# Decay scale of the recurrence: from short operations on DVE between weight halves to a chain on GpSimd between its loads and its copies

## The chip, the core and the metric

The kernel runs on one core of a Trainium2 chip. The metric is the device time of one execution in microseconds, as the median of a few runs. The engines are TensorE (PE), VectorE (DVE), ScalarE (ACT), GpSimd (POOL) and SyncE (SP), which here only issues DMAs. Each engine runs its own instructions in order, and they meet only through semaphores: an instruction adds to one when it is done (`then_inc`), another waits for a value (`wait_ge`).

## What is computed

Two model blocks run one behind the other on 256 tokens of width 1024: a gated linear recurrence with an attention layer of a sliding window, then two feed-forward parts around two kinds of attention. Everything this text speaks of lies at the start, in the recurrence:

```python
u = rmsnorm(x, norm_g) @ w_in                       # x: 256 x 1024, w_in: 1024 x 3072
xb, gate = u[..., :1536], u[..., 1536:]
xb = causal_depthwise_conv(xb, conv_w, conv_b)      # 4 taps
r = sigmoid(blockwise(xb, wr) + br)                 # 16 blocks of 96 x 96
i = sigmoid(blockwise(xb, wi) + bi)
log_a = -8.0 * r * softplus(-lam)                   # lam: 1536 numbers
a = exp(log_a)
b = sqrt(-expm1(2.0 * log_a)) * (i * xb)
hs = scan(a, b);  y = hs * silu(gate);  x = x + y @ w_out
```

The decay scale is the factor `-8 * softplus(-lam) / 2`, one number for each of the 1536 channels, so 12 for each of the 128 partitions. The kernel works it out once, as `softplus(-lam) = max(-lam, 0) + log(1 + e)` with `e = exp(-|lam|)`, and the logarithm as a series in `z = e / (2 + e)`.

## The kernel before

The time goes into matmuls with weights of 32 bits. Each weight half (128 partitions x 1024 columns, 512 KB) is loaded by SP's queue into `stage`. ACT copies it in rounded form to `w_hi` (function `hi`), and DVE subtracts, `w_lo = stage - w_hi` (function `lo`, L1729). PE multiplies each product in three passes: `w_hi` by the high part of the activations, `w_hi` by their low part, `w_lo` by the high part (L595). Halves are numbered through the whole program; four of them have room in the ring `w_hi`/`w_lo`. `ring_free` says that PE is done with a half, `hi_done` that ACT's part is there, `w_done` that DVE's is.

The recurrence layer runs so. PE makes `xb` in six chunks of two 128-channel tiles (chunk `c`, two halves each). ACT moves the result out of PSUM with the first tap, DVE adds the other three taps (L1942, six instructions of about 0.4 us for a chunk), ACT writes the high part (`xb_hi`), DVE the low part (`xb_lo`, L1734). The 96-wide blocks of the gate weights don't fit 128-wide tiles. So they come in four groups of three tiles (`gates(g)` on PE): for each group two halves of 768 columns, which hold the gate weights. The halves of groups 0 and 1 are in `gate_st`, those of groups 2 and 3 in `arena`. Part of the input channels has to be brought to other partitions: that is POOL's function `stack(g)`, eight copies (L487) that wait one for another (semaphore `stack_done`) and, at their start, for `xbl` (DVE's low parts). PE's `gates(g)` first does 18 matmuls that need no stacked channels, then waits for `stack_done >= 8 * (g + 1)` and does 12 more (L825 and L827). Only behind these come the matmuls of the next chunk.

POOL's program around the change is: clear the gate buffers, issue the DMAs of the gate weights of groups 0 and 1 (L495, L503), then the first part of those of groups 2 and 3 (L495), `stack(0)`, `stack(1)`, the rest of the DMAs for groups 2 and 3 (L503) and 14 small DMAs, `stack(2)`, a square of the decay (L525), `stack(3)`.

DVE's program is a loop over halves, `for n in range(half_of(C_G + 2))`, written out by hand. In turn `n` it does `xb_lo` where a chunk ended one turn before, the taps where a chunk ends (`n` = 1, 3, 5, 7, 11, 15), `lo(n + 4)`, and then some of the decay scale's operations: `lam_ratio` in turns 3 to 5, `lam_series` in turns 6 to 10. There are 15 of them on DVE, all 128x12, and each waits for the one before (`lam_step`). ACT delivers `e` (semaphore `lam_e`) in its turn 2, and needs the finished factor (`lam_ready`) in its turn 12.

Of the kernel before, what the change touches and what calls it, by code (L numbers as in the profile page):

```python
# [11 lines left out]
ALU = mybir.AluOpType  # L12
# [9 lines left out]
LT = LRU // P  # L22
# [3 lines left out]
LRU_C = 8.0  # L26
# [49 lines left out]
CONV_W, CONV_B, BR, BI, LAM = 0, 48, 60, 72, 84  # L76
# [102 lines left out]
def build(nc, I, out):  # L179
    ctx = ExitStack()  # L180
    with ctx:
        def sb(name, shape, dt=F32):
            return ctx.enter_context(nc.sbuf_tensor(name, shape, dt))

        def sem(name):
            return ctx.enter_context(nc.semaphore(name))
# [14 lines left out]
        par_a = sb("par_a", [P, ROWS_A])  # L201
# [12 lines left out]
        lam = sb("lam", [P, 8, LT])  # L214
# [29 lines left out]
        def stacked(g, m):  # L244
# [16 lines left out]
        std_ready, rstd_ready, rb_ready, rb_sb = sem("std_ready"), sem("rstd_ready"), sem("rb_ready"), sem("rb_sb")  # L261
        xn_ready, xh_ready, xl_ready = sem("xn_ready"), sem("xh_ready"), sem("xl_ready")
        xh_second = sem("xh_second")
        par_t, par_ready, lam_e, lam_step, lam_ready = (
            sem(n) for n in ("par_t", "par_ready", "lam_e", "lam_step", "lam_ready"))
        conv_b, conv_s, conv_x, xbh, xbl = sem("conv_b"), sem("conv_s"), sem("conv_x"), sem("xbh"), sem("xbl")
        ri_sig = sem("ri_sig")
        lru_a, lru_t, lru_aa, lru_m, lru_s, lru_bx, lru_b, lru_h, lru_silu = (
# [204 lines left out]
        def _(pool):  # L473
# [7 lines left out]
            def stack(g):  # L481

                pool.wait_ge(xbl, (3 * g + 2) // 2 + 1)
                for i, (m, p, n, part, k, at) in enumerate(STACK):
                    if g or i:
                        pool.wait_ge(stack_done, len(STACK) * g + i)
                    pool.tensor_copy(stacked(g, m)[p:p + n, :], acts[at:at + n, 8 + 3 * g + k, part, :].bitcast(F32))\  # L487
                        .then_inc(stack_done, 1)

            for pair, place in enumerate((gate_st, gate_hi)):  # L490
                pool.wait_ge(set_done, 4 + pair)
                for w, name in enumerate(("a_gate_r_w", "a_gate_i_w")):
                    blocks = I[name][0].rearrange("(g b) i j -> b i g j", b=4)
                    for b, r, n, p, c in GATE_PIECES:
                        pool.dma_start(place[p:p + n, :, w, c:c + LB], blocks[b, r:r + n, 2 * pair:2 * pair + 2, :])\  # L495
                            .then_inc(gate_in[pair], 16)
                if pair == 1:
                    stack(0)
                    stack(1)
                for w, name in enumerate(("a_gate_r_w", "a_gate_i_w")):  # L500
                    blocks = I[name][0].rearrange("(g b) i j -> b i g j", b=4)
                    for b, r, n, p, c, j0, jn in GATE_AGAIN:
                        pool.dma_start(place[p:p + n, :, w, c:c + jn],  # L503
                                       blocks[b, r:r + n, 2 * pair:2 * pair + 2, j0:j0 + jn]).then_inc(gate_in[pair], 16)
# [1216 lines left out]
        def _(dve):  # L1721
# [149 lines left out]
                dve.wait_ge(xbh, c + 1)  # L1871
                low(8 + 2 * c, tiles(XB + 2 * c, 2), 2).then_inc(xbl, 1)

            e, den, z, z2, ser, big = (lam[:, j, :] for j in range(1, 7))

            def lam_after(step):

                dve.wait_ge(lam_step, step)

            def lam_ratio(n):  # L1880
                if n == 9:
                    dve.wait_ge(lam_e, 2)
                    dve.tensor_scalar(den, e, 2.0, 1.0, ALU.add, ALU.mult).then_inc(lam_step, 1)
                    dve.tensor_scalar(big, par_a[:, LAM:LAM + LT], -1.0, 0.0, ALU.mult, ALU.max).then_inc(lam_step, 1)
                if n == 10:
                    lam_after(2)
                    dve.reciprocal(z, den).then_inc(lam_step, 1)
                    lam_after(3)
                    dve.tensor_tensor(z, z, e, ALU.mult).then_inc(lam_step, 1)
                if n == 11:  # L1890
                    lam_after(4)
                    dve.tensor_tensor(z2, z, z, ALU.mult).then_inc(lam_step, 1)
                    lam_after(5)
                    dve.tensor_scalar(ser, z2, 1.0 / 15.0, 1.0, ALU.mult, ALU.mult).then_inc(lam_step, 1)

            def lam_series(n):
                if 12 <= n < 18:
                    lam_after(n - 6)
                    dve.scalar_tensor_tensor(ser, ser, 1.0 / (37 - 2 * n), z2, ALU.add, ALU.mult).then_inc(lam_step, 1)
                if n == 18:  # L1900
                    lam_after(12)
                    dve.scalar_tensor_tensor(ser, ser, 1.0, z, ALU.add, ALU.mult).then_inc(lam_step, 1)
                    lam_after(13)
                    dve.scalar_tensor_tensor(ser, ser, 2.0, big, ALU.mult, ALU.add).then_inc(lam_step, 1)
                if n == 19:
                    lam_after(14)
                    dve.tensor_scalar(lam[:, 7, :], ser, -LRU_C / 2, 1.0, ALU.mult, ALU.mult).then_inc(lam_ready, 1)

            x_end = {half_of(c) + 1: c for c in range(6)}
            def lru_gated(g):  # L1910

# [15 lines left out]
            for n in range(half_of(C_G + 2)):  # L1927
                if n - 1 in x_end:
                    xb_lo(x_end[n - 1])
                if n in (half_of(C_G) + 2, half_of(C_G + 1) + 2):  # L1930
                    gate_out((n - half_of(C_G)) // 4)
                if n in x_end:
                    c = x_end[n]
                    dve.wait_ge(conv_b, 2 * c + 2)
                    for tap in range(1, CONV):
                        for m in range(2):
                            t = 2 * c + m
                            x = tiles(XB + t)
                            if tap >= 2:
                                dve.wait_ge(conv_s, 4 * c + 2 * (tap - 2) + m + 1)  # L1940
                            w = CONV_W + (CONV - 1 - tap) * LT + t
                            dve.scalar_tensor_tensor(x[:, tap:T], bank[4 + c % 2][:, m * T:(m + 1) * T - tap],  # L1942
                                                     par_a[:, w:w + 1], x[:, tap:T], ALU.mult, ALU.add)\
                                .then_inc(conv_x if tap == CONV - 1 else conv_s, 1)
                    if c == 0:
                        lo(4)
                if n:
                    lo(n + 4)
                lam_ratio(n + 6)
                if n in (6, 7, 8):  # L1950
                    lam_series(2 * n)
                    lam_series(2 * n + 1)
                if n in (9, 10):
                    lam_series(n + 9)
                if n in (14, 16):
                    lru_gated(n // 2 - 7)
                if n in (18, 20):
                    lru_square(n // 2 - 9)
                if n == 20:
                    lru_gated(2)  # L1960
                if n == 23:
                    lru_square(2)
# [401 lines left out]
            for r in range(NH + 5):  # L2364
# [9 lines left out]
                if r < NH:  # L2374
                    n = r
# [13 lines left out]
                if 2 <= r < NH + 2:  # L2389
                    n = r - 2  # L2390
# [117 lines left out]
```

## Time and profile before

| | |
|---|---|
| median of 3 runs | 786.79 us (786.68 to 787.05) |
| the profiled execution's own time | 786.78 us |
| span of its trace | 784.9 us |
| PE busy | 776.7 us, 99% of the span |
| DVE busy | 585.6 us, 75% |
| ACT busy | 488.0 us, 62% |
| POOL busy | 106.9 us, 14%, nearly all of it in the first 200 us |

The time of an execution is 1.9 us longer than the span of its trace; what lies around the span is not in the trace. A group's or an instruction's row begins with its start and its duration. PE's instructions overlap: a matmul of 256 columns has a duration of 0.28 us in the records, but the next one starts 0.12 us behind it. So the busy share says little of PE, and short stops are read from the starts. Every stretch of this trace has the granted clock 1.00.

### The profile page before, as it was taken

The numbers are of one execution on the slowest core, as the hardware profiler recorded it, in microseconds if no ns is written. First come the engines' busy times: TensorE is split into PE (matmuls) and PEld (weight loads), VectorE is DVE, ScalarE is ACT, GpSimd is POOL, SyncE is SP. The second block draws the span as 40 slices with busy tenths as digits, with TensorE's granted clock in tenths as the row PEclk, the third lists the DMA queues.
The fourth block names the chain that finished last, engine by engine and source line by source line (L and its number), as shares of the span: only waits on it lengthen the run. The fifth ranks groups of instructions, "written<-read, shape, count | busy, mean of one in ns | idle before, by whom it ended". The sixth has DMA issues, their size and how long they took to land.

```text
span 784.9 us, 14573 instructions
## 1 busy us (share of the span) xinstructions
PE 776.7 (99%) x5321; PEld 711.4 (91%) x5321; DVE 585.6 (75%) x892; ACT 488.0 (62%) x761; POOL 106.9 (14%) x195
## 2 busy tenths in 40 slices
PE   9999999999999999999999999999999999999997
PEld 8999999998998888888888899999999888888885
DVE  5989997978868887776459664796588887787443
ACT  7799946788675655554346565764756665555334
POOL 9697100157100000000000031000000000000000
PEclk9999999999999999999999999999999999999999
DMA  8663565633646766666665544445555676665651
GB/s 264 188 181 118 171 212 161 211 112 110 188 126 181 226 191 187 187 195 202 190 189 163 185 147 151 127 144 161 182 165 157 195 213 189 195 184 184 195 178 54
DMA packets 101557, 136.57 MB, mean 174 GB/s; under 512 B 5320, under 2 KB 86912, under 8 KB 101504
## 3 DMA queue, kind: packets, MB, share of 16 engines
q1 hardware_dynamic: 99232, 133.23, 55.4%
q0 software_dynamic: 2112, 2.54, 1.3%
q8 instruction: 35, 0.57, 0.3%
q14 instruction: 18, 0.15, 0.1%
q10 hardware_dynamic: 160, 0.07, 0.1%
HBM read 134.78 MB, written 1.05 MB: 173 GB/s over the span
## 4 chain that ended last, share of the span: by engine, by line
PE 91%; DVE 4%; ACT 3%; issue 1%; DMA 0%; ACTq 0%
PE bank L595 30%; PE bank L658 20%; PE bank L660 11%; PE bank L603 8%; PE bank L704 8%; PE bank L751 5%; PE bank L752 3%; DVE w_lo L1729 2%; DVE arena L1942 1%; PE bank L945 1%; PE bank L927 1%; ACT arena L1216 1%; PE bank L952 1%; ACT w_hi L1216 1%; ACT acts L1216 1%
## 5 line engine op out<-in xcount | busy, mean ns | idle before, releaser
L1729 DVE TENSOR_TENSOR w_lo<-stage,w_hi 128x1024 fp32r<-128x1024 f32 x249 | 305.3, 1231 | 124.5 <-ACT w_hi L1216 123.9
L1216 ACT ACTIVATE w_hi<-stage 128x1024 fp32r<-128x1024 f32 (+1 forms) x251 | 262.5, 1052 | 117.5 <-PE bank L595 41.7
L595 PE MATMUL bank<-acts,w_hi 128*128 128x256 f32 x1520 | 277.6, 285 | 0.9 <-DVE w_lo L1729 0.4
L658 PE MATMUL bank<-acts,w_hi 128*128 128x512 f32 x704 | 244.8, 392 | 0.0
L595 PEld LDWEIGHTS bank<-acts,w_hi 128*128 128x128 f32 x1520 | 236.5, 192 | 3.6 <-issue 1.7
L595 PE MATMUL bank<-acts,w_lo 128*128 128x256 f32 x760 | 214.9, 283 | 0.0
L660 PE MATMUL bank<-acts,w_lo 128*128 128x256 f32 x704 | 197.2, 280 | 0.0
L658 PEld LDWEIGHTS bank<-acts,w_hi 128*128 128x128 f32 x704 | 131.7, 187 | 29.2
L595 PEld LDWEIGHTS bank<-acts,w_lo 128*128 128x128 f32 x760 | 145.6, 192 | 0.0
L660 PEld LDWEIGHTS bank<-acts,w_lo 128*128 128x128 f32 x704 | 133.1, 189 | 0.0
L1216 ACT ACTIVATE arena<-bank 128x512 f32<-128x512 f32 (+1 forms) x79 | 43.6, 561 | 63.6 <-PE bank L660 45.9
L603 PE MATMUL bank<-w_hi,acts 128*128 128x256 f32 (+1 forms) x320 | 71.8, 319 | 0.4 <-DVE w_lo L1729 0.4
L555 POOL TENSOR_SCALAR arena<-arena,rden 128x128 f32<-128x128 f32 (+1 forms) x44 | 23.5, 547 | 283.7 <-DVE rden L2106 283.1
L751 PE MATMUL bank<-acts,w_hi 128*128 (+1 forms) x176 | 61.1, 391 | 0.0
L1216 ACT ACTIVATE acts<-arena 128x512 fp32r<-128x512 f32 (+3 forms) x41 | 26.4, 644 | 53.2 <-DVE arena L2260 32.9
L1216 ACT ACTIVATE arena<-arena 128x512 f32<-128x512 f32 (+3 forms) x64 | 38.4, 605 | 29.7 <-DVE arena L2236 14.5
L603 PEld LDWEIGHTS bank<-w_hi,acts 128*128 128x128 f32 x320 | 52.2, 191 | 4.6 <-DVE w_lo L1729 0.8
L704 PE MATMUL bank<-w_hi,acts 128*128 128x512 f32 x176 | 54.4, 390 | 0.0
L603 PE MATMUL bank<-w_lo,acts 128*128 128x256 f32 (+1 forms) x160 | 50.4, 315 | 0.0
L752 PE MATMUL bank<-acts,w_lo 128*128 (+1 forms) x176 | 49.3, 280 | 0.0
L2228 DVE TENSOR_TENSOR arena<-arena,bank 128x512 f32<-128x512 f32 x44 | 30.2, 685 | 22.2 <-ACT arena L1216 22.2
L751 PEld LDWEIGHTS bank<-acts,w_hi 128*128 128x128 f32 x176 | 32.9, 187 | 7.2
(221 smaller groups left out, 810.2 us busy)
## 6 DMA issues: line engine op xcount, KB each, us to landing
stage<-ffn_w_gate SPq DMA_DIRECT2D x44, 512.0 KB, 4.2
stage<-ffn_w_up SPq DMA_DIRECT2D x44, 512.0 KB, 4.4
stage<-ffn_w_down SPq DMA_DIRECT2D x44, 512.0 KB, 3.8
stage<-w_in SPq DMA_DIRECT2D x40, 512.0 KB, 3.6
stage<-a_w_in SPq DMA_DIRECT2D x24, 512.0 KB, 4.6
stage<-b_w_in SPq DMA_DIRECT2D x16, 512.0 KB, 3.7
stage<-a_w_out SPq DMA_DIRECT2D x12, 512.0 KB, 3.7
stage<-b_w_out SPq DMA_DIRECT2D x8, 512.0 KB, 3.5
```

The source lines that it names most:

```text
L555: pool.tensor_scalar(s, s, rden[:, 2 * n + q:2 * n + q + 1], 1.0, ALU.mult, ALU.mult).then_inc(p_norm, 1)
L595: mm = pe.matmul(dst, w[:, slot, c:c + P], a[:, k, :] if isinstance(k, int) else a[:, bass.ds(k, 1), :], start=start and n == 0, stop=stop ...
L603: mm = pe.matmul(dst, a[:, k, tb * P:(tb + 1) * P], w[:, slot, c:c + n], start=start and i == 0, stop=stop and i == 2, skip_group_check=True)
L658: pe.matmul(two[p][:, m, :], w_hi[:, half % RING, c:c + P], wide(acts[:, k, :, :]), start=k == 0, stop=False, skip_group_check=True)
L660: mm = pe.matmul(two[p][:, m, 0:T], w_lo[:, half % RING, c:c + P], a_hi[:, k, :], start=False, stop=k == KD - 1, skip_group_check=True)
L704: mm = pe.matmul(token_bank(tb, h)[:, :], a[:, k, t], w[:, slot, c], start=False, stop=w is w_hi and a is a_hi, skip_group_check=True)
L751: pe.matmul(b[:, :], w_hi[:, half % RING, w], both, start=start, stop=False, skip_group_check=True)
L752: return pe.matmul(b[:, 0:T], w_lo[:, half % RING, w], high, start=False, stop=stop, skip_group_check=True)
L927: mm = pe.matmul(bank[score_bank(n + i)][:, c:c + w], q[r, t * T + c:t * T + c + P], k[r, 0:keys], start=True, stop=True)
L1216: return nc.scalar.activation(out_, in_, func, **kw)
L1729: dve.tensor_tensor(w_lo[:, n % RING, 0:w], src, w_hi[:, n % RING, 0:w].bitcast(F32), ALU.subtract)\
L2228: dve.tensor_tensor(y, y, two[ffn_two(n, j, u)][:, :, 0:T], ALU.add).then_inc(ff_add, 1)
```

## The change

The 15 operations on DVE go away except the reciprocal. That one stands in turn 5 now, behind `lo(9)`, and waits for POOL (`lam_den`). All the others are done by POOL in the new function `decay_scale()`, which is called once, between the DMAs of `pair == 1` and `stack(0)`. The steps are written with two-operand and one-operand instructions in place of the fused ones, so there are more of them: two before the reciprocal, 17 behind it. Each waits for its predecessor, by `pool.wait_ge(lam_step, ...)`.

```diff
@@ POOL @@
+            def decay_scale():
+                steps = [0]
+                def step(op):
+                    steps[0] += 1
+                    op.then_inc(lam_step, 1)
+                    pool.wait_ge(lam_step, steps[0])
+                e, den, z, z2, ser, big = (lam[:, j, :] for j in range(1, 7))
+                pool.wait_ge(lam_e, 2)
+                pool.tensor_scalar(den, e, 2.0, 1.0, ALU.add, ALU.mult).then_inc(lam_den, 1)
+                step(pool.tensor_scalar(big, par_a[:, LAM:LAM + LT], LRU_C / 2, 0.0, ALU.mult, ALU.min))
+                pool.wait_ge(lam_inv, 1)
+                step(pool.tensor_tensor(z, z, e, ALU.mult))
+                step(pool.tensor_tensor(z2, z, z, ALU.mult))
+                step(pool.tensor_scalar(ser, z2, 1.0 / 15.0, 1.0 / 13.0, ALU.mult, ALU.add))
+                for n in (11, 9, 7, 5, 3):
+                    step(pool.tensor_tensor(ser, ser, z2, ALU.mult))
+                    step(pool.tensor_scalar(ser, ser, 1.0 / n, 1.0, ALU.add, ALU.mult))
+                step(pool.tensor_tensor(ser, ser, z2, ALU.mult))
+                step(pool.tensor_scalar(ser, ser, 1.0, -LRU_C, ALU.add, ALU.mult))
+                step(pool.tensor_tensor(ser, ser, z, ALU.mult))
+                pool.tensor_tensor(lam[:, 7, :], ser, big, ALU.add).then_inc(lam_ready, 1)
...
                 if pair == 1:
+                    decay_scale()
                     stack(0)
                     stack(1)
@@ DVE, loop over n @@
                 if n:
                     lo(n + 4)
-                lam_ratio(n + 6)
-                if n in (6, 7, 8):
-                    lam_series(2 * n)
-                    lam_series(2 * n + 1)
-                if n in (9, 10):
-                    lam_series(n + 9)
+                if n == 5:
+                    dve.wait_ge(lam_den, 1)
+                    dve.reciprocal(lam[:, 3, :], lam[:, 2, :]).then_inc(lam_inv, 1)
```

POOL's program, from its last DMA of the gate weights to `stack(0)` and the start of `stack(1)` (`lam` is the small tile of the decay scale, `acts` the activations that PE reads). Before:

```order
L495 DMA arena<-a_gate_i_w 96x2x96
L487 CAST acts<-acts 32x256 [waits xbl]
L487 CAST acts<-acts 32x256 [waits stack_done] x3
L487 CAST acts<-acts 64x256 [waits stack_done] x4
L487 CAST acts<-acts 32x256 [waits stack_done,xbl]
```

And now (from the first of these rows to the fifth step; behind them the same pair of operations comes four times more, then the last four steps, and then `stack(0)` as before):

```order
L520 DMA arena<-a_gate_i_w 96x2x96
L501 ISA
L501 TENSOR_SCALAR lam<-lam 128x12 [waits lam_e]
L502 TENSOR_SCALAR lam<-par_a 128x12
L504 TENSOR_TENSOR lam<-lam 128x12 [waits lam_inv,lam_step]
L505 TENSOR_TENSOR lam<-lam 128x12 [waits lam_step]
L506 TENSOR_SCALAR lam<-lam 128x12 [waits lam_step]
L508 TENSOR_TENSOR lam<-lam 128x12 [waits lam_step]
L509 TENSOR_SCALAR lam<-lam 128x12 [waits lam_step]
```

`stack(0)` stood directly behind the DMAs; now 19 operations on `lam` stand ahead of it, and the third of them waits for DVE's reciprocal.

DVE's program, turns 4 to 6 of its loop (`gate_st` rows are `lo(8)` and `lo(9)`). Before:

```order
L1734 TENSOR_TENSOR acts<-arena,acts 128x2x256 [waits xbh]
L1729 TENSOR_TENSOR w_lo<-gate_st,w_hi 128x768 [waits hi_done]
L1887 RECIPROCAL lam<-lam 128x12 [waits lam_step]
L1889 TENSOR_TENSOR lam<-lam 128x12 [waits lam_step]
L1942 SCALAR_TENSOR_TENSOR arena<-bank,par_a,arena 128x255 [waits conv_b]
L1942 SCALAR_TENSOR_TENSOR arena<-bank,par_a,arena 128x255
L1942 SCALAR_TENSOR_TENSOR arena<-bank,par_a,arena 128x254 [waits conv_s] x2
L1942 SCALAR_TENSOR_TENSOR arena<-bank,par_a,arena 128x253 [waits conv_s] x2
L1729 TENSOR_TENSOR w_lo<-gate_st,w_hi 128x768 [waits hi_done]
L1892 TENSOR_TENSOR lam<-lam 128x12 [waits lam_step]
L1894 TENSOR_SCALAR lam<-lam 128x12 [waits lam_step]
L1734 TENSOR_TENSOR acts<-arena,acts 128x2x256 [waits xbh]
```

And now:

```order
L1760 TENSOR_TENSOR acts<-arena,acts 128x2x256 [waits xbh]
L1755 TENSOR_TENSOR w_lo<-gate_st,w_hi 128x768 [waits hi_done]
L1933 SCALAR_TENSOR_TENSOR arena<-bank,par_a,arena 128x255 [waits conv_b]
L1933 SCALAR_TENSOR_TENSOR arena<-bank,par_a,arena 128x255
L1933 SCALAR_TENSOR_TENSOR arena<-bank,par_a,arena 128x254 [waits conv_s] x2
L1933 SCALAR_TENSOR_TENSOR arena<-bank,par_a,arena 128x253 [waits conv_s] x2
L1755 TENSOR_TENSOR w_lo<-gate_st,w_hi 128x768 [waits hi_done]
L1942 RECIPROCAL lam<-lam 128x12 [waits lam_den]
L1760 TENSOR_TENSOR acts<-arena,acts 128x2x256 [waits xbh]
```

The reciprocal moved behind a chunk's six taps and the second gate half: from in front of the first L1942 here to the place where L1892 stood. PE's and ACT's programs have the same instructions in the same order as before.

## Rows read from the trace of the kernel before

**Rows 1.** The page's first part: busy time, share of the span, instructions.
```profile
PE 776.7 (99%) x5321; PEld 711.4 (91%) x5321; DVE 585.6 (75%) x892; ACT 488.0 (62%) x761; POOL 106.9 (14%) x195
```

**Rows 2.** Waits of the weight loads, 16 to 130 us: total, times, longest.
```profile
PEld bank L595 <- DVE w_lo L1729: 0.8, 2, 0.6
```

**Rows 3.** PE in order of time, around its two stops.
```profile
41.61 0.28 PE L595 MATMUL bank<-acts,w_lo 128*128 128x256 f32 x1
41.95 0.50 PE L595 MATMUL bank<-acts,w_hi 128*128 128x256 f32 x2
...
60.99 0.28 PE L595 MATMUL bank<-acts,w_lo 128*128 128x256 f32 x1
61.65 0.50 PE L595 MATMUL bank<-acts,w_hi 128*128 128x256 f32 x2 [0.38 <-DVE w_lo L1729]
```

**Rows 4.** PE where `gates(0)` begins its last 12 matmuls.
```profile
37.41 0.28 PE L825 MATMUL bank<-acts,w_hi 128*128 128x256 f32 x1
```

**Rows 5.** POOL in order of time; idle time in brackets.
```profile
30.95 5.13 POOL L487 CAST acts<-acts 32x256 fp32r<-32x256 f32 x8 [5.94 <-DVE acts L1734]
36.69 5.46 POOL L487 CAST acts<-acts 32x256 fp32r<-32x256 f32 x8 [0.61 <-DVE acts L1734]
```

**Rows 6.** DVE in order of time, turns 3 to 6.
```profile
30.05 0.17 DVE L1883 TENSOR_SCALAR lam<-lam 128x12 f32<-128x12 f32 x1
30.20 0.69 DVE L1734 TENSOR_TENSOR acts<-arena,acts 128x512 fp32r<-128x512 f32 x1
...
31.67 0.22 DVE L1887 RECIPROCAL lam<-lam 128x12 f32<-128x12 f32 x1
32.01 2.42 DVE L1942 SCALAR_TENSOR_TENSOR arena<-bank,par_a,arena 128x255 f32<-128x255 f32 x6
...
35.22 0.40 DVE L1892 TENSOR_TENSOR lam<-lam 128x12 f32<-128x12 f32 x1
35.73 0.90 DVE L1734 TENSOR_TENSOR acts<-arena,acts 128x512 fp32r<-128x512 f32 x1
36.55 1.21 DVE L1729 TENSOR_TENSOR w_lo<-stage,w_hi 128x1024 fp32r<-128x1024 f32 x1
```

**Rows 7.** POOL, other stretches: short operations, and copies behind one another.
```profile
155.46 0.18 POOL L561 COPY arena<-sink 128x1 f32<-128x1 f32 x1
155.72 0.41 POOL L574 TENSOR_SCALAR arena<-con 128x256 f32<-128x256 f32 x1
71.09 1.47 POOL L525 TENSOR_TENSOR arena<-arena 128x768 f32<-128x768 f32 x1
30.95 2.43 POOL L487 CAST acts<-acts 32x256 fp32r<-32x256 f32 x4 [5.94 <-DVE acts L1734]
30.95 1.05 POOL L487 CAST acts<-acts 32x256 fp32r<-32x256 f32 x1 [5.94 <-DVE acts L1734]
36.69 1.33 POOL L487 CAST acts<-acts 32x256 fp32r<-32x256 f32 x1 [0.61 <-DVE acts L1734]
```

**Rows 8.** ACT in order of time.
```profile
24.24 0.21 ACT L1216 ACTIVATE lam<-lam 128x12 f32<-128x12 f32 x1
35.95 1.01 ACT L1216 ACTIVATE arena<-bank,par_a 128x256 f32<-128x256 f32 x2
40.63 0.63 ACT L1216 ACTIVATE acts<-arena 128x512 fp32r<-128x512 f32 x1 [2.72 <-DVE arena L1942]
```

**Rows 9.** PE's first matmuls, in order of time.
```profile
3.08 1.06 PE L783 MATMUL bank<-ones 128*128 128x128 f32 x4
5.93 0.87 PE L794 MATMUL bank<-con,arena 128*128 128x128 f32 x5
6.42 0.82 PE L794 MATMUL bank<-con,arena 128*128 128x128 f32 x6
```

**Rows 10.** All instructions of these lines: duration in ns, least/median/most.
```profile
L783 PE MATMUL bank<-ones x22: 275/421/581, 1.0 to 8.1; 128*128 128x128 f32 x22
L794 PE MATMUL bank<-con,arena x16: 272/273/474, 5.2 to 7.4; 128*128 128x128 f32 x16
```

More of the change, by code:

```diff
@@ L263, in build @@
         xh_second = sem("xh_second")
-        par_t, par_ready, lam_e, lam_step, lam_ready = (
-            sem(n) for n in ("par_t", "par_ready", "lam_e", "lam_step", "lam_ready"))
+        par_t, par_ready, lam_e, lam_den, lam_inv, lam_step, lam_ready = (
+            sem(n) for n in ("par_t", "par_ready", "lam_e", "lam_den", "lam_inv", "lam_step", "lam_ready"))
         conv_b, conv_s, conv_x, xbh, xbl = sem("conv_b"), sem("conv_s"), sem("conv_x"), sem("xbh"), sem("xbl")
@@ L1872, in xb_lo @@
                 low(8 + 2 * c, tiles(XB + 2 * c, 2), 2).then_inc(xbl, 1)
[L1874 to L1907, printed above, removed]
             x_end = {half_of(c) + 1: c for c in range(6)}
```

## The prediction

> **What bounds the kernel now.** I read the busy shares first: PE is at work for 776.7 us of the span and DVE for 585.6 [rows 1], so time is lost or won only where PE starts late. The waits of PE's weight loads come next. Between 16 and 130 us, the stretch of the changed code, PE stopped twice for `w_lo`, 0.8 us together [rows 2]. In PE's order of time the size of both is seen by the starts, which are 0.12 us apart for each matmul when nothing is late: from 41.61 the next would start at 41.73 and starts at 41.95, 0.22 us late; from 60.99 it would be 61.11 and is 61.65, 0.54 us late [rows 3]. So 0.76 us is all that lighter work on DVE can give back here, however much it is lighter.
>
> The opposite question is what can make PE late. POOL's order of time shows it: `stack(0)` starts at 30.95, when DVE's low parts are there, and takes 5.13 us, to 36.08 [rows 5]. PE reaches the matmuls that wait for it at 37.41 [rows 4]. That is a margin of 1.3 us, on an engine that looks idle at 14% busy. The gap of 5.94 us before `stack(0)` [rows 5] ends where `stack(0)` begins, so what is put there must be done by about 31, or by 32.3 with the margin.
>
> **The change part by part.** *When the chain on POOL can go on.* Two of its operations need only ACT's `e`, which is there at 24.45 [rows 8], and fall into the gap, at no cost. The third waits for DVE's reciprocal, and DVE has this now in turn 5, where L1892 stood: 35.22 in this trace [rows 6]. DVE gets there earlier by what is taken out before: two operations of `lam`, from 30.05 to 30.20, 0.15 us, and the reciprocal with the product, from 31.67 to 32.01, 0.34 us [rows 6]. So the reciprocal starts at 34.73 and is done, at 0.22 us [rows 6], at 34.95. By then the time at which `stack(0)` used to be three quarters done has passed, and 17 steps follow.
>
> *What a step costs.* POOL has no 128x12 operation in the trace. The lower bound is a copy of one column, 0.18 us. The upper one is a dependent copy of 256 columns in `stack(0)`: four took 2.43 and the first of them 1.05, so 0.46 us each [rows 7]. A 256-column operation lasts 0.41 [rows 7], so the wait between two steps is 0.05. The number of columns matters little at 12: (0.41 - 0.18) x 12/255 is 0.01 for one operand, (1.47 - 0.18) x 12/767 is 0.02 for two [rows 7]. I take 0.18 + 0.05 + 0.02 = 0.25 us, near the lower bound, since 12 columns are nearer to one than to 256. Alone, 17 steps would take 4.3 us.
>
> *What stands in their way.* The first copy of `stack(1)`, 0.41 us of work, took 1.33 us from 36.69 [rows 7], while DVE was in L1729 from 36.55 for 1.21 us, and the first copy of `stack(0)` took 1.05. The reverse is seen at 35.22 and 35.73, where DVE's 0.17 us operation took 0.40 and L1734 0.90 instead of 0.69 [rows 6] beside POOL's last copies. So POOL and DVE's instructions with two inputs in SBUF exclude one another, and POOL gets about one operation in at each boundary. The Trainium skill, GPSIMD Engine Reference, section "Key points", says that GpSimd shares its SBUF interfaces with VectorE and contends with instructions that have two SBUF inputs. By that rule the steps stop under L1734 and L1729, and the trace agrees with the 1.33 us; without it the chain would end 3 us sooner (a rival below).
>
> DVE after the reciprocal: `xb_lo(2)` 34.95 to 35.6, `lo(10)` to 36.75, six taps to 39.1 (2.4 us, input in PSUM, not in the way; ACT's first tap at 35.95 [rows 8] would be half a microsecond sooner), `lo(11)` to 40.3, `xb_lo(3)` to 40.95. POOL's steps: one at 35.6, nine in the 2.35 us of taps, one at 40.3, the last six behind 40.95, 1.5 us: the chain ends at 42.45. DVE is idle by then, since `lo(12)` needs a slot of the ring that PE holds. So `stack(0)` runs unhindered, 8 x 0.46 = 3.7 us, to 46.2.
>
> *PE's stop.* PE gets to L825 at 37.41 as before and stands until 46.2: 8.8 us. Behind the waiting matmul everything of PE is queued, and ACT and DVE wait for the ring in turn. Nothing of it comes back later, since PE is busy to the end. The two stops of before go away, 0.76 us: DVE is done with `lo(11)` long before, and the second one came from ACT, which waited 2.72 us for DVE's taps before 40.63 [rows 8] and now has time to spare. `stack(1)` follows `stack(0)` in about 5.4 us [rows 5], to 51.6, and `gates(1)` needs it some 9.4 us behind `gates(0)`, since PE's order between the two is unchanged. `lam_ready` comes at 42.45, while ACT needs it only behind work that waits for PE; it costs nothing.
>
> *PE after the stop.* No stretch of this trace shows a granted clock under 1.00. But PE's own rows show two paces. In its first microseconds, coming from idle, four records of 128 columns took 1.06 us, so (1.06 - 0.42)/3 = 0.21 us apart; from 6.42 on six took 0.82, (0.82 - 0.27)/5 = 0.11 apart [rows 9, 10]. That is the ratio of the two levels, 1.2 and 2.4 GHz. PE had worked since 1.00, and the five records from 5.93, at 0.15 apart [rows 9], straddle the change. So a slow stretch of about 5.2 us, which costs half of itself, 2.6 us. An 8.8 us stop is longer than any that this trace has behind the start; that the clock falls in it is an estimate from the start alone. Bounds: nothing, and 2.6 plus the same spread again if the rise comes late, 3.5 us. I take 2.6. The Trainium skill, "TensorE: Matmul & The Clock Gate", section "What's actually happening", says the array is at half its clock by default and that activity releases it; by that rule the price is paid after this stop too, and the start of this trace agrees.
>
> *Sum.* The profiled execution took 786.78 us, 0.01 from the median of 786.79. 786.8 + 8.8 - 0.8 + 2.6 = 797.4 us.
>
> **Rivals.**
> - *POOL and DVE don't hinder each other here.* The steps run from 35.0 to 39.3, `stack(0)` takes 3.7 to 5.13, the stop ends between 43.0 and 44.4, so it is 5.6 to 7.0 us long. Time: 786.8 + 6.3 - 0.8 + 2.6 = 794.9. Against it: the 1.33 and 0.40 us rows.
> - *A step costs as much as a copy of `stack`, 0.46 us.* One at 35.6, five in the taps, one at 40.3, ten behind 40.95: 45.55, and 49.3 with `stack(0)`, a stop of 11.9. Time 800.5. For it: each step is a round trip through a semaphore, which I priced from one pair of rows.
> - *The clock stays up.* The same stop without 2.6: 794.8.
> - *The other side, faster.* If `stack(0)` were done by 37.41, only the 0.76 us would count and the time would be 786.0. With 3.7 us for the copies the chain must end by 33.7, and at 17 steps of 0.25 the reciprocal must be done by 29.4. In DVE's order it stands behind `lo(9)`, at 34.95. Even steps that cost nothing would put the end at 38.7, 1.3 us late. It needs an order other than the printed one.
> - *Code for the arithmetic has to be loaded on POOL.* The program has an instruction L501 ISA in front of the first step. The Trainium skill, GPSIMD Engine Reference, section "Instruction dispatch", has an instruction-memory load of about 6 us at the first call of a freshly loaded kernel. In the two operations before the reciprocal it would be hidden by the gap from 25 to 34.95; only paid at the first two-operand step would it count. Worked from rows, bounded by the gap before `stack(0)`, 5.94 us [rows 5], as a length that the present order can hide: 797.4 + 5.9 = 803.3.
>
> **How the numbers follow.** Forecast as worked out 0.60; POOL unhindered 0.13; dear steps 0.12; clock stays up 0.10; code load 0.02; faster 0.02; none of these 0.01. The single time is that of the forecast, 797.4. The range, 792.8 to 801.0, holds the forecast, nearly all of the first and third rivals, and dear steps; outside are the code load, a short stop joined with a high clock (786.8 + 5.6 - 0.8 = 791.6) and the faster side. A change within 0.2% (1.6 us) can't be told from none. Slower by more than that: 0.96. Within it: 0.02. Faster by more than that would need 1.6 us, where 0.76 can be had: 0.02 for what I have overlooked.
>
> **What would show it.** PE's starts jump once, at L825 in `gates(0)`, from about 37.4 to about 46, released by POOL's `stack(0)`. POOL's `lam` operations: two near 25, then nothing until about 35, then 17 with holes under DVE's L1755 and L1760. PE's granted clock is under 1.00 in the microseconds behind the stop and the starts are 0.21 apart there. The stops of before at 41.95 and 61.65 have no counterpart. From there to the end each row stands later by the same amount. It would be wrong if `stack(0)` still ended before 37.41, if the steps ran evenly through L1755, if a second stop came at `gates(1)`, `gates(2)` or `gates(3)`, or if later stretches gave the time back.

## The result and the profile after

| | before | after |
|---|---|---|
| median | 786.79 us (786.68 to 787.05) | 796.35 us (795.76 to 796.73) |
| profiled execution | 786.78 us, span 784.9 | 795.76 us, span 794.0 |

The changed kernel is slower: the ratio is 1.0121, 95% interval 1.0106 to 1.0136. Its page begins with these lines (busy time, share, instructions), which answer to [rows 1]:

```profile
PE 777.4 (98%) x5321; PEld 712.4 (90%) x5321; DVE 583.8 (74%) x878; ACT 488.3 (62%) x761; POOL 112.6 (14%) x214
```

PE does the same work, DVE 1.8 us less, POOL 5.7 more. Nothing of 9 us is to be seen there; it is in where PE stands still. First its waits over the whole execution (total, times, longest), which answer to [rows 2]:

```profile
PE bank L851 <- POOL acts L487: 8.4, 1, 8.4
```

Then its instructions in order of time, which answer to [rows 3, 4]. L851 is L825 of before, L621 is L595:

```profile
37.09 0.28 PE L621 MATMUL bank<-acts,w_lo 128*128 128x256 f32 x1
45.80 0.58 PE L851 MATMUL bank<-acts,w_hi 128*128 128x256 f32 x1 [8.43 <-POOL acts L487]
46.18 0.41 PE L853 MATMUL bank<-acts,w_lo 128*128 128x256 f32 x1
46.40 0.41 PE L851 MATMUL bank<-acts,w_hi 128*128 128x256 f32 x1
```

One stop, at the place where `gates(0)` waits for `stack(0)`: due at 37.21, begun at 45.80, 8.59 us late. The next matmul starts 0.38 us behind it, and from there on the starts are 0.21 us apart where they should be 0.12. The granted clock (the first number behind the engines' busy times) says why:

```profile
42.00:43.00 1.00, 0.00 (x0) 0.00 (x0) 0.00 (x0) 0.00 (x0) 0.93 (x3) 0.74 1.02 358
43.00:44.00 1.00, 0.00 (x0) 0.00 (x0) 0.00 (x0) 0.00 (x0) 0.81 (x4) 0.50 0.08 27
...
49.00:49.20 0.20, 0.20 (x3) 0.20 (x3) 0.20 (x1) 0.20 (x1) 0.20 (x1) 0.50 0.00 0
49.20:49.40 0.20, 0.20 (x3) 0.20 (x3) 0.18 (x1) 0.20 (x1) 0.20 (x1) 0.74 0.00 0
49.40:49.60 0.20, 0.20 (x4) 0.20 (x4) 0.00 (x0) 0.20 (x1) 0.20 (x1) 1.00 0.00 0
```

It fell to the half level, 1.2 GHz, in the middle of 42 to 43 us, while PE stood, and rose near 49.3. POOL's order of time shows what PE waited for; these answer to [rows 5, 7]:

```profile
26.57 0.27 POOL L502 TENSOR_SCALAR lam<-par_a 128x12 f32<-128x12 f32 x1
34.89 0.46 POOL L504 TENSOR_TENSOR lam<-lam 128x12 f32<-128x12 f32 x1 [8.05 <-DVE lam L1942]
35.43 1.24 POOL L505 TENSOR_TENSOR lam<-lam 128x12 f32<-128x12 f32 x1
36.76 0.20 POOL L506 TENSOR_SCALAR lam<-lam 128x12 f32<-128x12 f32 x1
37.04 0.22 POOL L508 TENSOR_TENSOR lam<-lam 128x12 f32<-128x12 f32 x1
...
39.10 1.05 POOL L509 TENSOR_SCALAR lam<-lam 128x12 f32<-128x12 f32 x1
40.23 0.53 POOL L508 TENSOR_TENSOR lam<-lam 128x12 f32<-128x12 f32 x1
...
42.01 0.21 POOL L513 TENSOR_TENSOR lam<-lam 128x12 f32<-128x12 f32 x1
42.16 7.95 POOL L487 CAST acts<-acts 32x256 fp32r<-32x256 f32 x16
```

POOL stood 8.05 us for the reciprocal, did its 17 steps from 34.89 to 42.2, and then began the copies that used to begin at 30.95. DVE's rows, which answer to [rows 6]:

```profile
34.52 0.22 DVE L1942 RECIPROCAL lam<-lam 128x12 f32<-128x12 f32 x1
34.66 0.63 DVE L1760 TENSOR_TENSOR acts<-arena,acts 128x512 fp32r<-128x512 f32 x1
35.38 1.23 DVE L1755 TENSOR_TENSOR w_lo<-stage,w_hi 128x1024 fp32r<-128x1024 f32 x1
```

**The account.** I take for each PE instruction between 17 and 150 us how much later it started than 0.12 us for each matmul behind the one before. In the kernel before the two stops come to 0.95 us (0.76 at the stops, 0.19 more at the instructions just behind them). In the one after they are gone, the new stop is 8.59 and the slow stretch 1.63. PE also reached this part 0.2 us earlier (17.70 in place of 17.90). -0.95 + 8.59 + 1.63 - 0.2 = 9.07 us; the spans differ by 9.1. So in the profiled execution nothing is left to explain, and nothing was given back later. The median is 0.6 us longer than this execution. The spans of the other three are 0.4 to 0.8 us longer, at mean granted clocks of 0.992 to 0.994 where this one has 0.995; they left no trace that would show where.

### The profile page after: what moved, and what is told of

Its sections match the earlier page's. It is cut to its first block, busy times and chain, and to the rows that moved or that the text cites. A ratio compares the mean times of both kernels' runs of the same rounds, so it can differ in the third digit from the quotient of the medians.

```text
span 794.0 us, 14579 instructions
## 1 busy us (share of the span) xinstructions
PE 777.4 (98%) x5321; PEld 712.4 (90%) x5321; DVE 583.8 (74%) x878; ACT 488.3 (62%) x761; POOL 112.6 (14%) x214
## 3 DMA queue, kind: packets, MB, share of 16 engines
HBM read 134.78 MB, written 1.05 MB: 171 GB/s over the span
## 4 chain that ended last, share of the span: by engine, by line
PE 93%; DVE 3%; ACT 1%; POOL 1%; DMA 1%; issue 1%; SPq 0%; ACTq 0%; POOLq 0%
PE bank L621 32%; PE bank L684 20%; PE bank L686 11%; PE bank L629 8%; PE bank L730 8%; PE bank L777 5%; PE bank L778 3%; PE bank L971 1%; PE bank L953 1%; DVE w_lo L1755 1%; PE bank L978 1%; ACT acts L1242 1%; DMA arena<-x 1%; DVE arena L1933 1%; PE bank L851 0%
## 5 line engine op out<-in xcount | busy, mean ns | idle before, releaser
L621 PE MATMUL bank<-acts,w_hi 128*128 128x256 f32 x1520 | 277.6, 285 | 0.4 <-DVE acts L1867 0.3
L621 PEld LDWEIGHTS bank<-acts,w_hi 128*128 128x128 f32 x1520 | 236.9, 192 | 2.7 <-issue 1.7
L621 PE MATMUL bank<-acts,w_lo 128*128 128x256 f32 x760 | 215.1, 283 | 0.0
L621 PEld LDWEIGHTS bank<-acts,w_lo 128*128 128x128 f32 x760 | 145.8, 192 | 0.0
L778 PE MATMUL bank<-acts,w_lo 128*128 (+1 forms) x176 | 49.3, 280 | 0.0
```

Of the source, the lines that this page charges most:

```text
L621: mm = pe.matmul(dst, w[:, slot, c:c + P], a[:, k, :] if isinstance(k, int) else a[:, bass.ds(k, 1), :], start=start and n == 0, stop=stop ...
L778: return pe.matmul(b[:, 0:T], w_lo[:, half % RING, w], high, start=False, stop=stop, skip_group_check=True)
```

## The experiments

**The reciprocal sooner, twice.** The first theory was that the loss is the lateness of `stack(0)` and nothing else. The edit in the changed kernel (the second one has `n == 2`):

```diff
-                if n == 5:
+                if n == 3:
                     dve.wait_ge(lam_den, 1)
                     dve.reciprocal(lam[:, 3, :], lam[:, 2, :]).then_inc(lam_inv, 1)
```

Turn 3:

> Edit: the changed kernel with DVE's reciprocal in turn 3 of its loop in place of turn 5 (about 29.8 in place of 34.5 us). Nothing else moves. Theory (PE waits for stack(0), which waits for the 17 steps): the steps start near 30.1, one gets in at each boundary of DVE's two-input instructions and eight in the taps, the chain ends near 37.9, stack(0) near 42.4, PE's stop at gates(0) is about 5.2 us in place of 8.6. Time 791.1 us if TensorE's clock stays up, 792.7 if it falls (in the changed kernel it fell 5.3 us into the stop, so this is at the edge). Rival (the loss comes from the POOL operations as such or from POOL hindering DVE, wherever they stand): time stays near 796.

Turn 2:

> Edit: the changed kernel with DVE's reciprocal in turn 2 of its loop (about 26.6 us, just after POOL's first operation). Theory: the chain starts near 26.9 and ends near 33.1, stack(0) near 37.6 to 38.2, PE's stop is 0.4 to 1.0 us, the clock stays up, and the two old stops are gone (0.95): time 786.2 to 787.5, most likely 786.7, so no difference from before. Rival (the steps cost by themselves): near 796. If the steps hinder DVE as well, its weight halves come late and stops appear at 41 or 61 us: 787.5 to 789.

Measured: 794.43 us for turn 3 (1.0095, interval 1.0078 to 1.0111), 791.51 for turn 2 (1.0061, 1.0044 to 1.0078). Each move forward made it faster with the same operations on the same engines, so the rival that these cost about 9 us wherever they stand falls. But both sizes were missed, the second by nearly 5 us. PE's stop was 6.21 us in the one and 4.27 in the other, against 5.2 and 0.4 to 1.0 expected. POOL's rows of turn 2 show the reason:

```profile
28.49 0.20 POOL L509 TENSOR_SCALAR lam<-lam 128x12 f32<-128x12 f32 x1
28.78 2.76 POOL L508 TENSOR_TENSOR lam<-lam 128x12 f32<-128x12 f32 x1
31.62 0.20 POOL L509 TENSOR_SCALAR lam<-lam 128x12 f32<-128x12 f32 x1
...
33.66 1.69 POOL L512 TENSOR_TENSOR lam<-lam 128x12 f32<-128x12 f32 x1
35.43 0.21 POOL L513 TENSOR_TENSOR lam<-lam 128x12 f32<-128x12 f32 x1
```

and DVE's rows beside them:

```profile
28.79 1.21 DVE L1755 TENSOR_TENSOR w_lo<-stage,w_hi 128x1024 fp32r<-128x1024 f32 x1
29.92 0.68 DVE L1760 TENSOR_TENSOR acts<-arena,acts 128x512 fp32r<-128x512 f32 x1
30.52 0.94 DVE L1755 TENSOR_TENSOR w_lo<-gate_st,w_hi 128x768 fp32r<-128x768 f32 x1
31.39 2.42 DVE L1933 SCALAR_TENSOR_TENSOR arena<-bank,par_a,arena 128x255 f32<-128x255 f32 x6
```

A step of 0.21 us took 2.76: it met three DVE instructions with two inputs in SBUF that stand back to back, and waited for all three, to 31.46. It did not get in at the boundary of two of them, as the prediction had supposed. The next hold, 1.69 us, is two such instructions long (33.73 to 35.27). In the taps L1933, which read PSUM, steps go by at 0.29 us each.

The clock was the other miss. It fell in both kernels, and in turn 3 the slow stretch cost 2.59 us, in turn 2 1.56. Account: -0.95 + 6.21 + 2.59 = 7.85 against spans 7.9 apart; -0.95 + 4.27 + 1.56 - 0.23 (an earlier start) = 4.65 against 4.7.

**Ten steps fewer.** In `decay_scale()`:

```diff
-                for n in (11, 9, 7, 5, 3):
+                for n in ():
```

> Leaves out the five pairs of operations of the series' loop (so the decay scale is another number); 7 steps behind the reciprocal in place of 17. Theory: ten steps of 0.29 us and the hole of about 1.2 us among them go, the chain ends near 38.2, stack(0), now hindered by DVE's two-input instructions at 38.9 to 40.7, near 43.4: stop 6.2 us, the clock falls late in it and costs about 1 us: 793.0 us. Rival (the round trip to DVE's reciprocal and the first load of the arithmetic cost most, the steps little): 795 to 796.

Measured: 794.06 us (1.0092, 1.0075 to 1.0109), stop 6.09, slow stretch 1.85, -0.95 + 6.09 + 1.85 = 6.99 against 7.0. The chain ended at 38.34 in place of 42.22, 3.9 us sooner, and the stop is 2.5 us shorter: `stack(0)` began under DVE's two-input instructions now and took 5.1 us, where it took 3.6 when DVE was idle. The time is 1.1 us over the one expected, of which the clock is 0.85 (1.85 and not 1). Ten of the 17 steps taken out gave back 2.3 of the 9.6 us. With seven left PE still stood for 6 us, because the chain still begins only at 35.1, behind the reciprocal; the move of the reciprocal to turn 2, with all 17 steps, gave back 4.8.

**PE kept at work in the stop.** Between PE's first matmuls of `gates(0)` and its wait, PE multiplies ones by ones (`warm(36)`; the trace shows each call as two records). The result is not used:

```diff
+                if g == 0:
+                    pe.wait_ge(conv_x, 6)
+                    warm(36)
                 pe.wait_ge(stack_done, len(STACK) * (g + 1))
```

> Edit: the changed kernel, with 36 matmuls of ones by ones (128 columns, their result unused, as at the program's start) on TensorE between the first 18 matmuls of gates(0) and its wait for stack(0). They take about 7.9 us of the 8.6 us stop. Theory (the stop costs 8.6 us and 1.6 us more because the clock falls in it): PE goes on at 45.8 as before, granted clock 1.00 throughout, time 796.35 - 1.6 = 794.7 us. Rival (the 1.6 us behind the stop are another start-up cost, or the clock is nothing to the time): 796.3. If stack(0) is what PE waits for, the time can't fall under 794.5.

Measured: 795.82 us (1.0113, 1.0096 to 1.013). The clock part of the theory is borne out: it is 1.00 in every stretch from 17 to 130 us, also behind the stop. The time is not: 795.82 where 794.7 was expected, since two other things happened. PE's rows:

```profile
37.40 8.20 PE L809 MATMUL bank<-ones 128*128 128x128 f32 x72
46.59 0.39 PE L854 MATMUL bank<-acts,w_hi 128*128 128x256 f32 x1 [0.99 <-POOL acts L487]
...
70.95 0.50 PE L621 MATMUL bank<-acts,w_hi 128*128 128x256 f32 x2 [0.72 <-DVE w_lo L1758]
```

One POOL step was held for 1.95 us instead of 1.05 and the useful matmuls were due at 37.40 and came at 46.59, 9.19 us late. And a stop of 0.98 us at `lo(19)` came back, at the place of the old one at 61.65. DVE needed 2.20 us for this half, where it took 0.94 in the changed kernel, next to a POOL operation that had begun 0.08 us sooner:

```profile
68.62 1.46 POOL L551 TENSOR_TENSOR arena<-arena 128x768 f32<-128x768 f32 x1
68.70 2.20 DVE L1758 TENSOR_TENSOR w_lo<-arena,w_hi 128x768 fp32r<-128x768 f32 x1
```

-0.95 + 9.19 + 0.1 + 0.98 = 9.3 us, as the spans are apart. So the slow stretch went away as the theory has it, and two holds between POOL and DVE, of 0.6 and 0.98 us, took its place. This run shows that the clock falls because PE stands, and it does not show by itself what the fall costs: that is read from the starts of the matmuls in the other traces.

**The steps behind the copies.** The first two operations stay in the gap, the other 17 go behind `stack(1)`. The function is split in two (`next(scale)` is the first two operations, `next(scale, None)` the 17 steps), and the steps wait for the last copy:

```diff
-                    decay_scale()
+                    scale = decay_scale()
+                    next(scale)
                     stack(0)
                     stack(1)
+                    next(scale, None)
```

> Edit: the changed kernel with the two first POOL operations in the gap as now, but the 17 steps behind stack(0) and stack(1), ahead of POOL's further DMAs. Theory (only the place of the steps costs): PE goes through gates(0) at 37.4 without a stop; the steps run from about 42 to 48 us, lam_ready is 1 to 2 us late for ACT, the gate weights' last DMAs land near 57 where ACT wants them at 55, and stack(2) ends near 65.5 where PE wants it at 62.7: one or more new stops near 61 to 66 us of 2 to 4 us together, 789 to 790.5 us. Rival (17 operations on POOL cost their time wherever they stand): 795 to 796.

Measured: 796.16 us (1.0124, 1.0108 to 1.0139), as slow as the changed kernel and 6 us over the theory. By the number alone the rival had won, and only the trace says otherwise: PE goes through `gates(0)` without a stop and has two others. Its waits:

```profile
PE bank L855 <- POOL acts L487: 3.3, 1, 3.3
PE bank L625 <- DVE w_lo L1759: 3.1, 1, 3.1
```

The second of these begins in ACT's program:

```profile
45.77 1.06 ACT L1246 ACTIVATE w_hi<-stage 128x1024 fp32r<-128x1024 f32 x1
51.33 3.07 ACT L1246 ACTIVATE arena<-arena,lam 128x256 f32<-128x256 f32 x6 [4.49 <-POOL lam L515]
```

ACT stood 4.49 us for the decay scale, which was ready at 51.3; I had put it at about 48. The copies are why. The steps could begin only at 44.47, since `stack(1)`, which ended at 42.15 in the kernel before, ended at 44.4 here. One of its copies, begun at 39.16, was held by four DVE instructions with two inputs in SBUF that follow one another at once:

```profile
39.16 3.84 POOL L487 CAST acts<-acts 64x256 fp32r<-64x256 f32 x1
```

```profile
39.20 1.21 DVE L1759 TENSOR_TENSOR w_lo<-stage,w_hi 128x1024 fp32r<-128x1024 f32 x1
40.33 0.68 DVE L1764 TENSOR_TENSOR acts<-arena,acts 128x512 fp32r<-128x512 f32 x1
40.93 1.81 DVE L1759 TENSOR_TENSOR w_lo<-gate_st,w_hi 128x768 fp32r<-128x768 f32 x2
```

In the kernel before, two short operations stand behind the first of these four (at 41.82) and two behind the third (at 43.77). With ACT stood the rounded weight halves behind it in ACT's queue, so PE stood 3.30 us at 57.26. The other is `stack(2)`, behind POOL's DMAs, 3.46 us at 70.21. Slow stretches of 1.54 and 1.49 us follow. -0.95 + 3.30 + 1.54 + 3.46 + 1.49 = 8.8 of 9.0.

**The gap used for DMAs.** As before, with POOL's eight DMAs of gate weights (4.5 us) moved from behind `stack(1)` to the gap ahead of `stack(0)`:

```diff
+                    next(scale)
                 for w, name in enumerate(("a_gate_r_w", "a_gate_i_w")):
...
+                if pair == 1:
+                    stack(0)
+                    stack(1)
+                    next(scale, None)
```

> Edit: as the one before, and in the gap before stack(0) POOL issues the eight DMAs of gate weights (4.5 us) that came behind stack(1). Theory: stack(0) starts near 31.3 in place of 30.95 and is inside its margin; the weights land early; the steps end near 48, the small DMAs and stack(2) come as early as before; ACT gets lam_ready up to 1.5 us late, which can leave one stop of 0 to 1 us near 61. Time 785.9 to 786.8, most likely 786.3, so the gain of at most 0.95 us at last, or no difference. Rival: 788 or more, if POOL's steps hinder DVE's weight halves behind 42 us.

Measured: 791.09 us (1.0056, 1.0042 to 1.007), over 4 us more than expected. The stop for `stack(2)` is gone, the one for ACT's `lam_ready` is the same 3.30 us (the copy of 3.84 us is here too, at 39.22), and one of 1.78 us appeared at 65.97, for `lo(19)`; -0.95 + 3.30 + 0.07 + 1.78 + 0.10 = 4.3, as the spans. So the 17 steps cost 4.3 us here and 9.6 in the changed kernel, by who waits behind them. No place I tried on POOL is free.

**How much DVE's relief is worth.** In the kernel before, DVE does one of its 15 operations:

```diff
-                lam_ratio(n + 6)
-                if n in (6, 7, 8):
-                    lam_series(2 * n)
-                    lam_series(2 * n + 1)
-                if n in (9, 10):
-                    lam_series(n + 9)
+                if n == 10:
+                    dve.wait_ge(lam_e, 2)
+                    dve.tensor_scalar(lam[:, 7, :], lam[:, 1, :], -LRU_C / 2, 1.0, ALU.mult, ALU.mult).then_inc(lam_ready, 1)
```

> Leaves out the decay scale's series: DVE does one operation in turn 10 in place of 15, so the factor is another number. Upper bound of what taking the work off DVE can give. Theory: the two stops go and nothing else changes, 785.8 us (0.95 less than before). Rival (DVE's 3 us of short operations are worth their time): 783.8.

Measured: 786.93 us (ratio 1.0003, 0.9994 to 1.0012). Neither theory holds. The two old stops are gone as I said, and three others have come, 0.28 at 37.59, 0.57 at 71.99 and 0.30 at 76.61, which with -0.95 make the 0.2 us by which the spans differ. Two of them are PE waiting for POOL's copies:

```profile
37.29 0.28 PE L595 MATMUL bank<-acts,w_lo 128*128 128x256 f32 x1
37.59 0.39 PE L825 MATMUL bank<-acts,w_hi 128*128 128x256 f32 x1
...
71.99 0.39 PE L825 MATMUL bank<-acts,w_hi 128*128 128x256 f32 x1 [0.31 <-POOL acts L487]
```

POOL's copies of `stack(0)` in this kernel, and DVE's rows beside them:

```profile
33.75 3.33 POOL L487 CAST acts<-acts 64x256 fp32r<-64x256 f32 x2
```

```profile
33.86 0.94 DVE L1729 TENSOR_TENSOR w_lo<-gate_st,w_hi 128x768 fp32r<-128x768 f32 x1
34.73 0.68 DVE L1734 TENSOR_TENSOR acts<-arena,acts 128x512 fp32r<-128x512 f32 x1
35.59 1.22 DVE L1729 TENSOR_TENSOR w_lo<-stage,w_hi 128x1024 fp32r<-128x1024 f32 x1 [0.18 <-ACT w_hi L1216]
```

Two copies of 0.41 us took 3.33. In the kernel before, the two at the same place (34.36) took 1.72, and there DVE had its short operations between L1729 and L1734 [rows 6]. From this comes a theory: the work taken off DVE was also what let POOL in.

**The same with turns 5 and 6 moved.** In the kernel before, nothing left out:

```diff
-                lam_ratio(n + 6)
+                lam_ratio({3: 9, 4: 10, 7: 11}.get(n, 0))
+                for k in {7: (12, 13), 8: (14, 15, 16), 9: (17, 18), 10: (19,)}.get(n, ()):
+                    lam_series(k)
```

> Edit: the kernel before, all of the decay scale on DVE, but the two operations of turn 5 and the two of turn 6 moved to turn 7 and behind (turn 7: four, turn 8: three, turn 9: three, turn 10: one), so that they follow lo(11) instead of preceding it. Theory (the two stops of the kernel before come from DVE's 1.5 us of short operations ahead of lo(11)): PE's stop at 41.95 goes away, ACT gets chunk 3 about 1 us sooner, the stop at 61.65 shrinks or goes: 785.8 to 786.2 us. Rival (the stops come from ACT or from POOL's use of the port): 786.8 as before.

Measured: 787.15 us, so slower, if by little (1.0011, 1.0002 to 1.002). The stop at 41.95 is gone, one of 0.30 at 37.60 is there, and the one of 61.65 is 0.97 in place of 0.64: its `lo(19)` took 2.21 us, begun at 59.71 next to POOL's L525, where it took 1.30 before. Two of the 11 executions took 789.06 and 789.34 us, at a granted clock of 0.999 and more; none of these has a trace, and the median does not hang on them.

From these two I formed the theory of openings, and two kernels test it. One leaves turns 3 to 5 as they were and moves only turn 6's pair:

```diff
-                if n in (6, 7, 8):
-                    lam_series(2 * n)
-                    lam_series(2 * n + 1)
-                if n in (9, 10):
-                    lam_series(n + 9)
+                for k in {7: (12, 13, 14), 8: (15, 16, 17), 9: (18,), 10: (19,)}.get(n, ()):
+                    lam_series(k)
```

> Edit: the kernel before, with only the two operations of turn 6 moved to turns 7 and 8 (turn 7: three, turn 8: three, turns 9 and 10: one each); turns 3 to 5 keep their six. New theory (POOL's copies get the port only where DVE's two-input instructions don't follow one another at once, and the short operations of turns 3 to 5 are such places): stack(0) ends near 36.1 again, there is no stop at 37.6, lo(11) is 0.5 us sooner, so the stop at 41.95 goes, and the stop near 61.7 is between 0.1 and 1.0 us: 786.2 to 787.0. Old theory (every short operation off DVE's path ahead of lo(11) gains): 786.0. Rival (stack(0) is late in the two kernels before by chance): 787.1 as dve_later.

The other leaves out the series (the same five lines go) and keeps `lam_ratio` in turns 3 to 5:

```diff
+                if n == 10:
+                    lam_after(6)
+                    dve.tensor_scalar(lam[:, 7, :], ser, -LRU_C / 2, 1.0, ALU.mult, ALU.mult).then_inc(lam_ready, 1)
```

> Leaves out the decay scale's series from turn 6 on, as dve_light (so the factor is another number), but keeps the six short operations of turns 3 to 5 where they stood. New theory: these six work as openings for POOL's copies, so stack(0) ends near 36.1 and PE's stop at 37.6 (0.28 us in dve_light) is gone although DVE has more to do; the stop at 41.95 is gone too: 786.2 to 786.7, less than dve_light's 786.93 by 0.3 us or so. Rival (more work on DVE can only cost): 786.9 to 787.3.

Measured: 786.37 us for the first (0.9995, 0.9986 to 1.0004), 786.69 for the second (1.0, 0.9991 to 1.0009). In both, `stack(0)` takes 5.13 and 5.14 us as before, and there is no stop at 37.6 and none at 41.95; left are 0.53 and 0.89 us near 61.3. `stack(0)` of the first kernel, to be held against [rows 5]:

```profile
30.98 5.13 POOL L487 CAST acts<-acts 32x256 fp32r<-32x256 f32 x8 [5.96 <-DVE acts L1734]
```

For the traces this bears the theory out: with six more operations on DVE, the second kernel has lost `dve_light`'s stop at `stack(0)`. The two that count are those of turn 5, between L1729 and L1734: `dve_later` keeps turns 3 and 4 and has the stop, these two kernels keep turn 5 as well and don't. As times, 786.69 against 786.93 is no more than a leaning, since the two intervals overlap. The first, `dve_mid`, is the best kernel of the study: its 11 runs lie between 786.30 and 786.64, the 21 of the kernel before between 786.46 and 786.95. The interval of the ratio still includes 1. In its trace -0.95 + 0.53 is the 0.4 us by which its span is shorter.

## Why the prediction was right

797.4 us were predicted and 796.35 measured, in the range of 792.8 to 801.0. By its steps:

1. *POOL reaches the chain's third operation only behind DVE's turn 5, at 34.95.* Measured: the reciprocal ended at 34.74, in a trace that runs 0.2 us earlier there. Right.
2. *A step costs 0.25 us.* Measured 0.20 to 0.22 as duration and 0.29 from start to start. Too cheap by 0.04, for 17 steps 0.7 us.
3. *DVE's two-input instructions hold the chain; it ends at 42.45.* It ended at 42.22. That it comes so near is luck, since two errors cancel: of 7.5 us in all I had 3.25 for holds, and the four long steps show 0.25 + 1.03 + 0.85 + 0.32 = 2.45 (over 0.21 each). The mechanism as I put it, one operation at each boundary, was wrong where several such instructions follow one another (2.76 us for one step with the reciprocal in turn 2). In the changed kernel it happened to matter little: eight of the 17 steps fell into the taps, and five came when DVE was done (from 40.85).
4. *`stack(0)` runs unhindered, 3.7 us.* Measured 3.6 (42.16 to 45.8), and DVE was idle from 40.7 to 48.4. Right.
5. *A stop of 8.8 us, one place.* 8.59 us, at L851. Right.
6. *A slow clock behind it, 2.6 us.* Right in kind, 1.0 us too dear in the profiled execution: 1.63. This is the term that was mis-sized. It was read from one slow stretch of 5.2 us at the start [rows 9, 10]. But the clock fell at 42.5, while PE still stood, and rose at 49.3, so only 3.5 us of PE's work, from 45.8, ran slow. Where PE worked longer before the rise, it cost more: 4.1 us for 1.85 in `short_series`, 5.7 us for 2.59 in `recip_turn3` (rises at 47.55 and 49.34). The other stops cost 1.56, 1.54 and 1.49, and in `dmas_in_gap` nothing.
7. *The old stops go, 0.76 us, and nothing comes back.* 0.95 with the instructions just behind them. That ACT and DVE were ahead of PE during the stop is seen in DVE's idle time of 7.73 us before 48.42. The later rows are all 9.1 us later.

The sum was 10.6 us over before; the profiled execution is 9.0 over and the median 9.6. Step 6 is 1.0 of the difference, steps 5 and 7 are 0.2 each, the earlier start of PE is 0.2.

The rivals: that POOL and DVE don't hinder one another is refuted by 1.24 and 1.05 us for single steps. Steps of 0.46 are refuted by 0.29. The clock did fall. There was no load of code in the chain: behind the wait, the first arithmetic with two operands took 0.46 us, and the operation at 25.11, the first on POOL, 1.39, both far below the 5.9 us of that rival, the latter inside the gap.

What the text took for granted and the runs don't bear out stands in its first part: that 0.76 us is what lighter work on DVE gives back. DVE's short operations were not only a cost ahead of `lo(11)`; between two long instructions they also let POOL through. Without them, in `dve_light`, 0.95 us of old stops turned into 1.15 us of new ones.

What stays open is when the clock falls. `behind_stacks` and `dmas_in_gap` have nearly the same stop, and only in one did it fall (below). The traces show that it differs, not why. Open is also why executions of one kernel differ, by 1 us in the changed kernel and by 2.4 us in `dve_later`.

## What to carry to other kernels

An idle stretch of a helper engine has a deadline, which is what stands behind it in that engine's queue. Before work is put in, look for the last input it waits for, not only for its length: here a gap of 5.9 us was there for a chain whose input came 4 us after its end. Here an engine at 14% had 1.3 us of margin for 17 steps and became the one that PE waited for, while PE's two waits for the one at 75% had come to 0.8 us in this part [rows 2].

When instructions of two engines exclude one another, short operations between long ones are openings for the other engine. Taking them out can move the wait to the other side for nothing gained, so look at the neighbour's durations, not only at the relieved engine's.

A total time can hide two mechanisms: the chain in front of the copies and the chain behind them both cost 9.4 us or more, by stops at different places and with different causes. Write down the account of the stops for each kernel.

## What the runs showed of the hardware that I had not expected

One 128x12 step on POOL was held for as long as three DVE instructions with two SBUF inputs that followed one another without a gap (2.76 us), and not served between them; a copy was held for four (3.84 us, in three kernels). Elsewhere a held step did end with the first one of two (the one of 1.05 us at 39.10, beside an instruction to 40.09). Between 24 and 130 us the twelve traces have 36 POOL operations that were held by a run of two to four such DVE instructions (the subtractions for `w_lo` and for the low parts of the activations), and the start tells the two kinds apart. Eleven were held to the end of the run, and they had begun between 0.11 us before and 0.12 us behind the start of its first instruction. The other 25 got in behind the instruction that they had met, and they had begun 0.23 to 0.77 us behind the start of that one. So a POOL operation that arrives together with such a run waits for all of it, and one that arrives in its midst waits for one instruction. That is what was seen in each of the 36 cases; what makes it so is not shown.

TensorE's clock fell in the midst of the stops of 8.6, 6.2 and 6.1 us. With those of 4.3 us (`recip_turn2`) and 3.5 us (the second of `behind_stacks`) it fell only 0.4 and 0.7 us behind the moment when PE had begun to work again, at 41.8 and 70.9. And of two stops of 3.3 us in two kernels one was followed by the fall and the other was not. Each row is a stretch of 1 us, with the granted clock behind the engines' busy times; first `behind_stacks`, where PE stood from 53.96 to 57.26:

```profile
56.00:57.00 1.00, 0.00 (x0) 0.00 (x0) 1.00 (x1) 1.00 (x2) 1.00 (x3) 1.00 0.17 33
57.00:58.00 1.00, 0.74 (x3) 0.77 (x4) 1.00 (x2) 1.00 (x4) 1.00 (x3) 0.62 0.05 8
58.00:59.00 1.00, 1.00 (x7) 1.00 (x6) 0.25 (x1) 1.00 (x4) 1.00 (x3) 0.50 0.62 131
```

then `dmas_in_gap`, where it stood from 53.98 to 57.28:

```profile
57.00:58.00 1.00, 0.72 (x6) 0.75 (x7) 1.00 (x2) 1.00 (x4) 1.00 (x2) 1.00 0.03 1
58.00:59.00 1.00, 1.00 (x10) 1.00 (x10) 0.27 (x1) 1.00 (x4) 1.00 (x3) 1.00 0.79 194
```

With equal stops, and both at 1.00 before, the one ran at half its clock behind it and the other did not. In the first the clock fell as PE was taking up work again. So in these two kernels a stop of 3.3 us had a price of 1.54 us once and none once, from one trace of each.
